# A three-block transformer kernel: causal mask and row minimum of the attentions in one VectorE operation per head and tile, both heads' turned probabilities copied at once, forget logits on quarters of the array

## The chip, the cores and the metric

The kernel runs on one core of a Trainium2 chip. The metric is the device time of one execution in microseconds (us), lower is better. Before the change the median of three runs is 1467.6 us (1465.63 to 1467.93).

## What is computed

Three blocks are applied to 512 tokens of width 1024 in float32: a first block (a gated recurrence, a pooling branch, an MLP of width 4096), a second that mixes 8 heads of attention with a forget gate and 8 heads of retention ("even" in the code, the attention is called fox), and a third with 16 heads in three attention branches ("odd", called nsa). The change touches the softmax of the attentions and the forget gate's logits. Cut to what matters:

```python
# fox: 8 heads of 64, 512 tokens
c = jnp.cumsum(jax.nn.log_sigmoid(f_logit + b_f), axis=1)        # f_logit = h @ w_in[:, 1536:1544]
s = jnp.einsum('bhqd,bhkd->bhqk', qi, kh) * scale
s = s + ci[..., None] - c_h[:, :, None, :]
p = masked_softmax(s, key_pos[None, :] <= t[:, None])            # causal
o = jnp.einsum('bhqk,bhkd->bhqd', p, vh)
# nsa: 16 heads of 64; the selected blocks and the window both cover all 512 tokens here,
# so each of these two branches is a causal softmax with the slope of the head
s = jnp.einsum('bqghd,bgqld->bghql', qi, k_sel) * scale
s = s - slopes * (t[None, None, :, None] - tok)[:, :, None]
p = masked_softmax(s, (tok <= t[None, None, :, None])[:, :, None])
```

## The kernel before, in words

All five engines have an instruction list written out by hand (`@block.tensor` PE, `@block.vector` DVE, `@block.scalar` ACT, `@block.gpsimd` POOL, `@block.sync` SP), and counting semaphores order them. Activations lie in SBUF with 128 features or tokens on the partitions. PE multiplies most weights in three float16 passes (L739 to L741 with weights as the stationary side, L782 to L784 with activations there): a high half times a high half and the two mixed products. SP loads the weights into a ring of three slots, ACT measures (L1364) and makes the high half (L1347), POOL reduces the measure over partitions (L710), DVE makes the low half (L1976). That chain runs ahead of PE through the whole kernel.

`attention(A)` exists on PE, DVE and ACT and is called twice, for fox with 8 heads and one branch (12 steps) and for nsa with 16 heads and two branches (48 steps). A step is one pair of heads (e = 0, 1), one branch and one entry of `TILES`: query tile 3 with 512 keys, or tile 2 with 384 keys, or tiles 1 and 0 together with 256 and 128 keys. Three steps make a round. In each round of the loop over i:

- PE does the scores of step i into PSUM banks 0 to 3 (L960, L964; two slots, so it waits for the exponentials of step i-2), then turns the probabilities of step i-3 into banks 4 and 5, one bank per head (L982), then multiplies the turned probabilities of step i-4 with the values into banks 6 and 7 (L1000). In nsa the first step of a pair of heads also adds the compressed branch (L994).
- DVE adds the constant `future` (1e30 above the diagonal) to the last 128 keys of each tile in PSUM, one operation for both heads (L2521), waits for it, takes the minimum over the keys, again for both heads (L2525), and releases ACT. Scores are negated, so the minimum is the softmax's maximum. Then it takes the reciprocal of the sums of step i-1 (L2534) and scales that step's probabilities (L2543 in nsa, L2541 in fox). Once a pair of heads it multiplies the output by the gate (L2557) and makes a low half (L1890).
- ACT copies the turned probabilities of step i-3 from PSUM to SBUF, one operation per head (L1681), waits for DVE's minimum and makes the exponentials with their sums (L1690), one operation per head and tile.

The order within one engine is fixed by that loop, and the transposes of the two heads wait apart for "probabilities scaled" and "bank free":

```python
975   if TURN_LAG <= i < N + TURN_LAG:
976       s = i - TURN_LAG
977       for e in range(2):
978           pe.wait_ge(s_(n + "_pn"), n_(n + "_pn", 2 * s + e + 1))
979           if s >= 1:
980               pe.wait_ge(s_(n + f"_te{e}"), n_(n + f"_te{e}", s))
```

The forget logits (`fl`, L1217) are 8 columns of weights against 512 tokens: 24 matmuls with 8 stationary columns and 512 moving ones into one bank, and one ACT operation (L1630) that adds the bias. They stand between the projections `vf` and `qr`; the row that comes of them (`frow`) is used only by the fox attention, 100 us later.

## Time and profile before

| | |
|---|---|
| median of three runs | 1467.6 us (1465.63 to 1467.93) |
| the profiled execution | 1465.37 us, its span 1463.5 us |
| PE busy | 1430.4 us, 98% of the span |
| DVE busy | 955.3 us, 65% |
| ACT busy | 860.6 us, 59% |
| chain that ended last | PE 82%, DVE 13%, ACT 2%, issue 1%, DMA 1% |
| costliest lines in the chain | L739 to L741 14% each, L782 to L784 8% each, L2525 4%, L2543 2%, L2521 2% |
| the fox attention | starts at 980 us |
| the nsa attention | starts at 1265 us |

"Busy" is the time in which at least one instruction of the engine is under way. Times of PE are starts; their ends are modelled, so PE counts as busy through short gaps. The chain is followed back from the last instruction; where two engines are about equally loaded it can go through either.

### The profile page before, as it was taken

How to read it: one execution, taken by the hardware profiler on the slowest of the kernel's cores; microseconds unless marked ns; L12 is line 12 of the kernel's file. 1: busy time of each engine (PE TensorE's matmuls, PEld its weight loads, DVE VectorE, ACT ScalarE, POOL GpSimd, SP SyncE). 2: the span in 40 equal slices, each digit the busy share in tenths (PEclk: the TensorE clock that was granted, in tenths of full speed). 3: DMA queues.
4: the chain of work that ended last, by engine and by line, in shares of the span. 5: the costliest groups of instructions: out<-in, count | busy, mean ns of one | idle time of the engine just before them, and what ended most of it. 6: DMA issues, size and time to landing. Idle time of an engine off the chain costs nothing.

```text
span 1463.5 us, 24784 instructions
## 1 busy us (share of the span) xinstructions
PE 1430.4 (98%) x10076; PEld 924.8 (63%) x10076; DVE 955.3 (65%) x1926; ACT 860.6 (59%) x1241; POOL 63.6 (4%) x149
## 2 busy tenths in 40 slices
PE   7999999999999999999999999999999999899998
PEld 4444477556568548576688864746695855366677
DVE  6732556888679675555677524578667337799974
ACT  6554456777564665454563654457655466678863
POOL 0000000000000000000010000100100000000000
PEclk9999999999999999999999999999999999999999
DMA  6323223213332433433232332330223433100002
GB/s 195 107 95 113 88 87 97 76 59 115 100 102 87 136 113 98 141 112 113 95 108 67 113 110 87 96 108 1 61 87 116 144 110 98 58 2 2 2 3 100
DMA packets 128497, 131.85 MB, mean 90 GB/s; under 512 B 9896, under 2 KB 125392, under 8 KB 128256
## 3 DMA queue, kind: packets, MB, share of 16 engines
q1 hardware_dynamic: 126096, 121.62, 26.0%
q0 software_dynamic: 2288, 8.64, 1.7%
q8 instruction: 80, 1.31, 0.4%
q14 instruction: 33, 0.27, 0.1%
HBM read 128.12 MB, written 2.10 MB: 89 GB/s over the span
## 4 chain that ended last, share of the span: by engine, by line
PE 82%; DVE 13%; ACT 2%; issue 1%; DMA 1%; SPq 0%; DVEq 0%; POOL 0%; ACTq 0%
PE bank L739 14%; PE bank L741 14%; PE bank L740 14%; PE bank L782 8%; PE bank L783 8%; PE bank L784 8%; DVE tmin L2525 4%; DVE scr L2543 2%; DVE bank L2521 2%; PE bank L908 1%; PE bank L926 1%; DVE wring L1976 1%; PE bank L1063 1%; PE bank L1158 1%; PE bank L862 1%
## 5 line engine op out<-in xcount | busy, mean ns | idle before, releaser
L739 PE MATMUL bank<-xT,whigh 128*128 128x512 f16 x952 | 361.1, 379 | 0.3 <-DVE wring L1976 0.2
L741 PE MATMUL bank<-xT,wring 128*128 128x512 f16 x952 | 361.1, 379 | 0.0
L740 PE MATMUL bank<-xT,whigh 128*128 128x512 f16 x952 | 361.1, 379 | 0.0
L1976 DVE SCALAR_TENSOR_TENSOR wring<-wring,wsc,whigh 128x2048 f16<-128x2048 f32 (+2 forms) x106 | 245.2, 2313 | 137.1 <-ACT whigh L1347 136.5
L1347 ACT ACTIVATE whigh<-wring,wsc 128x2048 f16<-128x2048 f32 (+2 forms) x106 | 209.0, 1972 | 109.5 <-DVE wsc L1879 90.4
L1364 ACT ACTIVATE whigh<-wring 128x2048 bf16<-128x2048 f32 (+2 forms) x106 | 199.1, 1878 | 92.1 <-DMA wring<-in_w_down 31.2
L782 PE MATMUL bank<-whigh,slab 128*128 128x256 f16 x800 | 218.1, 273 | 1.8 <-DVE wring L1976 1.3
L783 PE MATMUL bank<-wring,slab 128*128 128x256 f16 x800 | 218.1, 273 | 0.0
L784 PE MATMUL bank<-whigh,slab 128*128 128x256 f16 x800 | 218.1, 273 | 0.0
L739 PEld LDWEIGHTS bank<-xT,whigh 128*128 128x128 f16 x952 | 93.2, 98 | 112.8 <-issue 2.7
L741 PEld LDWEIGHTS bank<-xT,wring 128*128 128x128 f16 x952 | 93.0, 98 | 112.5
L740 PEld LDWEIGHTS bank<-xT,whigh 128*128 128x128 f16 x952 | 93.0, 98 | 112.1 <-issue 2.6
L1869 DVE TENSOR_SCALAR wexp<-wexp 128x1 f32<-128x1 f32 x109 | 16.5, 152 | 161.3 <-POOL wexp L710 160.6
L710 POOL PARTITION_ALL_REDUCE wexp<-wsc x109 | 44.6, 410 | 1266.6 <-ACT whigh L1364 1259.8
L1283 ACT ACTIVATE slab<-bank,winv 128x256 f32<-128x256 f32 (+1 forms) x76 | 43.5, 572 | 91.7 <-PE bank L741 50.5
L782 PE MATMUL bank<-whigh,xT 128*128 128x256 f16 (+1 forms) x352 | 89.8, 265 | 0.0
L783 PE MATMUL bank<-wring,xT 128*128 128x256 f16 (+1 forms) x352 | 89.8, 265 | 0.0
L784 PE MATMUL bank<-whigh,xT 128*128 128x256 f16 (+1 forms) x352 | 89.8, 265 | 0.0
L782 PEld LDWEIGHTS bank<-whigh,slab 128*128 128x128 f16 x800 | 78.1, 98 | 12.5 <-issue 3.1
L783 PEld LDWEIGHTS bank<-wring,slab 128*128 128x128 f16 x800 | 78.1, 98 | 9.5
L784 PEld LDWEIGHTS bank<-whigh,slab 128*128 128x128 f16 x800 | 78.2, 98 | 9.2
L1690 ACT ACTIVATE scr<-bank,tmin 128x256 f32<-128x256 f32 (+2 forms) x120 | 61.9, 524 | 28.4 <-DVE tmin L2525 28.2
(335 smaller groups left out, 2270.2 us busy)
## 6 DMA issues: line engine op xcount, KB each, us to landing
wring<-in_w_in SPq DMA_DIRECT2D x27, 1024.0 KB, 5.1
wring<-in_w_up SPq DMA_DIRECT2D x16, 1024.0 KB, 5.4
wring<-in_w_down SPq DMA_DIRECT2D x16, 1024.0 KB, 5.4
wring<-in_even_w_in SPq DMA_DIRECT2D x14, 1024.0 KB, 5.4
wring<-in_odd_w_in SPq DMA_DIRECT2D x14, 1024.0 KB, 5.1
wring<-in_w_a SPq DMA_DIRECT2D x4, 1024.0 KB, 5.4
wring<-in_w_out SPq DMA_DIRECT2D x4, 1024.0 KB, 5.4
wring<-in_even_w_out SPq DMA_DIRECT2D x4, 1024.0 KB, 5.1
```

The costliest lines, as they stand in the source:

```text
L710: pool.partition_all_reduce(wexp[:, n:n + 1], wsc[:, n:n + 1], P, RMAX).then_inc(s_("w_all"), 1)
L739: pe.matmul(bank, wh[:, k, wcol:wcol + width], xh[:, k, :], start=k == 0, stop=False)
L740: pe.matmul(bank, wh[:, k, wcol:wcol + width], xl[:, k, :], start=False, stop=False)
L741: mm = pe.matmul(bank, wl[:, k, wcol:wcol + width], xh[:, k, :], start=False, stop=k == KC - 1)
L782: pe.matmul(bank, xh[:, k, tt], wh[:, k, 0:width], start=k == 0, stop=False)
L783: pe.matmul(bank, xh[:, k, tt], wl[:, k, 0:width], start=False, stop=False)
L784: mm = pe.matmul(bank, xl[:, k, tt], wh[:, k, 0:width], start=False, stop=k == KC - 1)
L1347: act.activation(high_of(i)[:, :, 0:m], loaded(i)[:, :, 0:m], ACT.Copy, scale=wsc[:, n:n + 1]).then_inc(s_("w_high"), 1)
L1364: act.activation(high_of(i)[:, :, 0:m].bitcast(BF16), loaded(i)[:, :, 0:m], ACT.Abs, accum_out=wsc[:, n:n + 1]).then_inc(s_("w_max"), 1)
L1690: ins = act.activation(probs(i, e, SEQ)[:, cc], scores(i, e)[:, cc], ACT.Exp, scale=-1.0, bias=pair_stat(tmin, i, part, e), accum_out=pair ...
L1976: dve.scalar_tensor_tensor(low_of(i)[:, :, 0:m], loaded(i)[:, :, 0:m], wsc[:, n:n + 1], high_of(i)[:, :, 0:m], ALU.mult, ALU.subtract).the ...
L2525: ins = dve.tensor_reduce(pair_stat(tmin, i, part), bank[:, 2 * (i % SCORE_SLOTS):2 * (i % SCORE_SLOTS) + 2, c:c + (t + 1) * P], AX_X, ALU ...
```

## The change

What it does:

- **Mask and minimum.** The constant `future` becomes 128 x 512, zeros in the first 384 columns and the old triangle in the last 128, and its last w columns fit a tile of w keys. One `tensor_tensor_reduce` per head and tile adds it to the scores in PSUM and gives the minimum. Each is two instructions on DVE, the operation and a read of the accumulator. The operation that masked and the one that reduced, each for both heads, go, and so does DVE's wait between them.
- **The constant** is loaded by POOL twice (once ahead of fox into `side` row 9, once ahead of nsa into row 14) and no longer by SP at the start.
- **Copies.** PE signals once when both heads are turned, ACT copies both banks in one operation, and PE waits for that copy before it turns the next step's first head.
- **Forget logits.** 96 matmuls with 8 stationary and 128 moving columns: token tile t goes to the array's columns from 32 t and to its own bank. Four ACT operations of 8 x 128 add the bias, and the bias is loaded by SP to four places.

```diff
-    c["future"] = ((p[None, :] > p[:, None]) * BIG).astype(np.float32)
+    c["future"] = np.concatenate([np.zeros((P, 3 * P)), (p[None, :] > p[:, None]) * BIG], 1).astype(np.float32)
...
-            (future[:, :], cd["future"]),
...
-            (bf_[:, :], a["even_b_f_2"][0].rearrange("(k p) -> k p", p=1)),
+            *((bf_[32 * t:32 * t + 8, :], a["even_b_f_2"][0].rearrange("(k p) -> k p", p=1)) for t in range(TT)),
...
+        future = {"fox": side[:, 9, :], "nsa": side[:, 14, :]}
...
+                    pool.dma_start(future["fox"], cd["future"]).then_inc(s_("decay_in"), 16)
...
+                    pool.dma_start(future["nsa"], cd["future"]).then_inc(s_("nsa_in"), 16)
...
+            def forget_tile(w):
+
+                (wh, wl), (xh, xl) = w, xhalves
+                for k in range(KC):
+                    for n, (ww, xx) in enumerate(((wh, xh), (wh, xl), (wl, xh))):
+                        for t in range(TT):
+                            mm = pe.matmul(SA[t][32 * t:32 * t + 8, 0:P], ww[:, k, 0:8], xx[:, k, t * P:(t + 1) * P],
+                                           start=k == 0 and n == 0, stop=k == KC - 1 and n == 2)
+                mm.then_inc(s_("fl_mm"), 1)
...
                         s = i - TURN_LAG
+                        if s >= 1:
+                            pe.wait_ge(s_(n + "_te"), n_(n + "_te", s))
                         for e in range(2):
                             pe.wait_ge(s_(n + "_pn"), n_(n + "_pn", 2 * s + e + 1))
-                            if s >= 1:
-                                pe.wait_ge(s_(n + f"_te{e}"), n_(n + f"_te{e}", s))
                             for j in range(width(steps[s][2]) // P):
                                 mm = pe.transpose(TPB[e][:, j * P:(j + 1) * P], probs(s, e, SEQ)[:, j * P:(j + 1) * P], ident[:, :])
-                            mm.then_inc(s_(n + f"_tp{e}"), 1)
+                        mm.then_inc(s_(n + "_tp"), 1)
...
-            feat_tile("fl", w, 0, xhalves, SA[0][0:8, :], width=8)
+            forget_tile(w)
...
-            ins = act.activation(frow[0], SA[0][0:8, :], ACT.Identity, bias=bf_[:, 0:1], scale=undo("fl", 0)[0:8, :])
+            for t in range(TT):
+                r = slice(32 * t, 32 * t + 8)
+                ins = act.activation(frow[0][:, t * P:(t + 1) * P], SA[t][r, 0:P], ACT.Identity, bias=bf_[r, 0:1], scale=undo("fl", 0)[r, :])
...
-                        for e in range(2):
-                            act.wait_ge(s_(n + f"_tp{e}"), n_(n + f"_tp{e}", s + 1))
-                            act.activation(turned_probs(s, e)[:, 0:w], TPB[e][:, 0:w], ACT.Copy).then_inc(s_(n + f"_te{e}"), 1)
+                        c = 2 * (s % TURNED_SLOTS)
+                        act.wait_ge(s_(n + "_tp"), n_(n + "_tp", s + 1))
+                        act.activation(xT[:, c:c + 2, 0:w], bank[:, 4:6, 0:w], ACT.Copy).then_inc(s_(n + "_te"), 1)
...
-                        for t, c in steps[i][2]:
-                            last = bank[:, 2 * (i % SCORE_SLOTS):2 * (i % SCORE_SLOTS) + 2, c + t * P:c + (t + 1) * P]
-                            ins = dve.tensor_tensor(last, last, future[:, :].unsqueeze(1).to_broadcast([P, 2, P]), ALU.add)
-                        ins.then_inc(dve_chain, 1)
-                        dve.wait_ge(dve_chain, own(dve_chain))
-                        for part, (t, c) in enumerate(steps[i][2]):
-                            ins = dve.tensor_reduce(pair_stat(tmin, i, part), bank[:, 2 * (i % SCORE_SLOTS):2 * (i % SCORE_SLOTS) + 2, c:c + (t + 1) * P],
-                                                    AX_X, ALU.min)
+                        for e in range(2):
+                            for part, (t, c) in enumerate(steps[i][2]):
+                                w = (t + 1) * P
+                                x = scores(i, e)[:, c:c + w]
+                                ins = dve.tensor_tensor_reduce(x, x, future[n][:, SEQ - w:SEQ], 1.0, BIG, ALU.add, ALU.min, pair_stat(tmin, i, part, e))
                         ins.then_inc(s_(n + "_dm"), 1)
```

Three places show how the instructions move. On DVE in the nsa attention, one step with 512 keys and the next with 384; `tmin` holds the minima, `trec` the reciprocals, `scr` and `side` the probabilities. Before:

```order
L2521 TENSOR_TENSOR bank<-bank,future 128x2x128
L2525 TENSOR_REDUCE tmin<-bank 128x2
L2534 RECIPROCAL trec<-tsum 128x4
L2543 TENSOR_SCALAR scr<-scr,trec,gates 128x256
L2543 TENSOR_SCALAR scr<-scr,trec,gates 128x128
L2543 TENSOR_SCALAR scr<-scr,trec,gates 128x256
L2543 TENSOR_SCALAR scr<-scr,trec,gates 128x128
L2521 TENSOR_TENSOR bank<-bank,future 128x2x128
L2525 TENSOR_REDUCE tmin<-bank 128x2
```

And in the changed kernel (`ISA` is the new operation or, without an input, its accumulator read):

```order
L2534 ISA bank,tmin<-bank,side 128x512
L2534 ISA tmin 128x1
L2534 ISA bank,tmin<-bank,side 128x512
L2534 ISA tmin 128x1
L2542 RECIPROCAL trec<-tsum 128x4
L2551 TENSOR_SCALAR scr<-scr,trec,gates 128x256
L2551 TENSOR_SCALAR scr<-scr,trec,gates 128x128
L2551 TENSOR_SCALAR scr<-scr,trec,gates 128x256
L2551 TENSOR_SCALAR scr<-scr,trec,gates 128x128
L2534 ISA bank,tmin<-bank,side 128x384
L2534 ISA tmin 128x1
L2534 ISA bank,tmin<-bank,side 128x384
```

Two instructions on 2 x 128 and 2 x 512 elements become four on 512, 1, 512 and 1; nothing else on DVE moves. On PE at the forget logits, before:

```order
L784 MATMUL bank<-whigh,xT 128x256
L739 MATMUL bank<-xT,gates 8x512
L740 MATMUL bank<-xT,gates 8x512
L741 MATMUL bank<-xT,gates 8x512
L739 MATMUL bank<-xT,gates 8x512
```

and in the changed kernel, where the projection `qr` follows at once:

```order
L795 MATMUL bank<-whigh,xT 128x256
L751 MATMUL bank<-xT,gates 8x128 x96
L740 MATMUL bank<-xT,whigh 128x512
L741 MATMUL bank<-xT,whigh 128x512
L742 MATMUL bank<-xT,wring 128x512
```

24 matmuls become 96 of a quarter of the length. On ACT in the nsa attention, before:

```order
L1690 ACTIVATE scr,tsum<-bank,tmin 128x128
L1681 ACTIVATE xT<-bank 128x512 x2
L1690 ACTIVATE scr,tsum<-bank,tmin 128x512 x2
L1681 ACTIVATE xT<-bank 128x384 x2
L1690 ACTIVATE side,tsum<-bank,tmin 128x384 x2
```

and in the changed kernel:

```order
L1701 ACTIVATE scr,tsum<-bank,tmin 128x128
L1692 ACTIVATE xT<-bank 128x1024
L1701 ACTIVATE scr,tsum<-bank,tmin 128x512 x2
L1692 ACTIVATE xT<-bank 128x2x384
L1701 ACTIVATE side,tsum<-bank,tmin 128x384 x2
```

The two copies of a step become one of twice the size in the same place of the queue.

## Rows read from the trace of the kernel before

**Rows 1.** 50 us of the nsa attention: busy us of PE, PEld, DVE, ACT, POOL; then clock
```profile
1300.00:1350.00 50.00, 50.00 (x486) 33.57 (x487) 48.69 (x115) 40.97 (x128) 0.00 (x0) 1.00 0.01 2
```
**Rows 2.** Chain that ended last, nsa attention: start, us, what
```profile
1299.68 0.61 DVE slab L2557
...
1370.16 0.61 DVE slab L2557
```
**Rows 3.** Timeline of DVE, one round: start, duration, line, operation
```profile
1338.92 0.42 DVE L2521 TENSOR_TENSOR bank<-bank,future 128x256 f32<-128x256 f32 x1
1339.38 1.23 DVE L2525 TENSOR_REDUCE tmin<-bank 128x2 f32<-128x1024 f32 x1
1340.52 0.17 DVE L2534 RECIPROCAL trec<-tsum 128x4 f32<-128x4 f32 x1
...
1341.89 0.43 DVE L2521 TENSOR_TENSOR bank<-bank,future 128x256 f32<-128x256 f32 x1
...
1343.22 0.15 DVE L2534 RECIPROCAL trec<-tsum 128x2 f32<-128x2 f32 x1
...
1344.33 0.76 DVE L2521 TENSOR_TENSOR bank<-bank,future 128x256 f32<-128x256 f32 x2
...
1346.07 0.15 DVE L2534 RECIPROCAL trec<-tsum 128x2 f32<-128x2 f32 x1
...
1347.04 0.42 DVE L2521 TENSOR_TENSOR bank<-bank,future 128x256 f32<-128x256 f32 x1
```
**Rows 4.** Timeline of PE in the nsa attention
```profile
1314.50 1.07 PE L994 MATMUL bank<-slab 31*64 31x512 f32 x4
...
1341.54 1.09 PE L1000 MATMUL bank<-xT,slab 128*64 128x128 f32 x16
1342.57 0.34 PE L960 MATMUL bank<-side 64*128 64x256 bf16 x4
...
1367.57 1.07 PE L994 MATMUL bank<-slab 31*64 31x512 f32 x4
```
**Rows 5.** Who waited for whom, 1290 to 1390 us: total, times, longest
```profile
PEld bank L982 <- DVE scr L2543: 2.3, 3, 0.8
...
PEld bank L960 <- ACT scr L1690: 0.7, 3, 0.4
```
**Rows 6.** Chain that ended last, fox attention
```profile
989.47 1.22 DVE tmin L2525
...
1007.60 1.23 DVE tmin L2525
```
**Rows 7.** Timeline of ACT in the nsa attention
```profile
1339.00 1.09 ACT L1681 ACTIVATE xT<-bank 128x512 f32<-128x512 f32 x2
1340.64 0.69 ACT L1690 ACTIVATE scr<-bank,tmin 128x512 f32<-128x512 f32 x1 [0.55 <-DVE tmin L2525]
...
1341.32 0.68 ACT L1690 ACTIVATE scr<-bank,tmin 128x512 f32<-128x512 f32 x1
```
**Rows 8.** Instructions of L2301, a running scan in the first block
```profile
L2301 DVE TENSOR_TENSOR_SCAN scr<-segment,scr x8: 1217/1224/1226, 228.4 to 354.9; 128x512 f32<-128x512 f32 x8
```
**Rows 9.** Instructions of L739 on the forget weights: ns least, median, most; first and last start
```profile
L739 PE MATMUL bank<-xT,gates x8: 378/379/380, 870.6 to 875.1; 128*8 128x512 f16 x8
```
**Rows 10.** Timeline of PE in a projection with 128 moving columns
```profile
809.82 0.22 PE L862 MATMUL bank<-xT,slab 128*128 128x128 f16 x1
809.87 0.22 PE L863 MATMUL bank<-xT,slab 128*128 128x128 f16 x1
```
**Rows 11.** Timeline of PE, end of the nsa attention
```profile
1410.35 1.01 PE L982 MATMUL bank<-ident,scr 128*128 128x128 f32 x6 [0.88 <-ACT xT L1681]
```
**Rows 12.** Timeline of POOL after the fox attention
```profile
1052.36 0.60 POOL L710 PARTITION_ALL_REDUCE wexp<-wsc  x1 [22.06 <-ACT whigh L1364]
```
**Rows 13.** Timeline of SP at the start
```profile
18.92 0.36 SPq L634 DMA_DIRECT2D bgate<-in_odd_b_gate  x1
22.89 36.81 SPq L622 DMA_DIRECT2D wring<-in_w_in  x5
```

21 lines of the change are left out of this document (9 added, 12 removed).

## Prediction, made before the changed kernel was run

> **What bounds the kernel now.** The page's table comes first: PE is busy 98% of the span, and the chain runs through it for 82%. So only two kinds of edit can count: one that takes PE time away, and one in a stretch where PE waits or its load is matched by another engine. The forget logits are of the first kind, the attentions of the second, since DVE's 13% of the chain lies mostly there.
>
> Next I read the busy times of a stretch within nsa [rows 1]: PE 50.00 of 50 us, DVE 48.69, ACT 40.97, clock 1.00. Two engines look full, and the question that decides this case is which one sets the pace. The chain goes through DVE, but a chain has to choose. So I measured the period of a pair of heads (two rounds, six steps) on both. DVE's output product comes at 1299.68 and, four pairs later, at 1370.16 [rows 2]: 70.48 / 4 = 17.62 us. PE's compressed-branch product comes at 1314.50 and, three pairs later, at 1367.57 [rows 4]: 53.07 / 3 = 17.69 us. They are equal to 0.4%. The waits agree: in 100 us PE's weight loads waited 2.3 us for DVE's scaled probabilities and 0.7 us for ACT [rows 5], and part of that is under matmuls still streaming. **PE is as full as DVE in nsa**: a faster DVE finds PE at 17.69 us a pair.
>
> Fox is different: the minimum of a pair's first step starts at 989.47 and, two pairs later, at 1007.60 [rows 6], 9.07 us a round. PE's need for a round without L994 follows from nsa: (17.69 - 1.0) / 2 = 8.34, with 1.07 for L994 [rows 4], of which about 1.0 is to the next start. So fox has 0.73 us a round of PE slack.
>
> **The mask and the minimum.** I take DVE's cost from start to start [rows 3]. Step with 512 keys: 1338.92 to 1340.52 = 1.60. Step with 384: 1341.89 to 1343.22 = 1.33. Step with 256 and 128: 1344.33 to 1346.07 = 1.74. Sum 4.67 us of the round of 8.12 (1338.92 to 1347.04). In these, the slope is one element in 1.04 ns, since the reduction of 1024 elements takes 1.14 us to the next start, 1.067 + 0.07. The round's reductions stream 2 x (512 + 384 + 256 + 128) = 2560 elements, 2.67 us, and the masks 1024 more.
>
> The new operations stream the same 2560 elements at best, in 8 operations with 8 accumulator reads. With o the overhead of one operation and its read, the new sum is 2.67 + 8 o, and **break-even is o = (4.67 - 2.67) / 8 = 0.25 us**. The trace has no such operation on DVE. Bounds from the nearest rows: two DVE instructions that don't wait for each other cost 0.07 each, so o = 0.14 at least. At most the read waits until its operation has ended: the reduction of 1024 lasts 1.23 where it streams 1.067 [rows 3], 0.16 over, and a small instruction lasts 0.15, so o = 0.31. The nearest row is ACT's, which has the very pair: an exponential of 512 with its read takes 1341.32 - 1340.64 = 0.68 to the next start, while two copies of 512 without a read last 1.09 together, 0.545 each with the tail of the second [rows 7]. So a read costs ACT 0.14 or a little more. With DVE's 0.07 for the operation that is 0.21, and I take o = 0.2.
>
> DVE then needs 2.67 + 1.6 = 4.27 a round, 0.4 less. In nsa that buys almost nothing, as PE holds 17.69 a pair: I count 0.5 us for PE's visible waits [rows 5] (0 to 0.7). In fox three of the four rounds run in the steady order: 3 x 0.4 = **-1.2** (0 to -2.2, by the 0.73). At the start of each attention DVE's minimum stands alone in the way (nothing is yet there for PE to do), and about 0.25 us each is saved: **-0.5** for both (0 to -0.8). The Trainium skill, in VectorE: DVE Perf Modes, section Rules for kernel authors, speaks against the change: don't fuse chained DVE operations for speed, since the pipeline drains after each, but minimise their number. Here DVE's instructions for mask and minimum rise from 8 to 16 a round; by that rule alone DVE would lose, which is the second rival's time.
>
> **The copies.** ACT's work shrinks by some 0.06 us a step, and ACT is 82% busy in nsa [rows 1]: nothing. But the copy now starts after both heads are turned. In the steady order PE has a product and the scores of the next step between (1341.54 to 1342.57 is the product alone [rows 4]), so the wait is covered by at least 1.7 us of PE work, against 1.0 us of copy; if DVE became late, it would still be covered. At the end of an attention that cover is gone: PE already waits 0.88 us for the first head's copy there [rows 11], and will wait for the whole of it, some 0.45 us more (half of the 1.09 of both copies [rows 7]), twice with a smaller tile after. I count **+0.5** for each attention, +1.0 (0.3 to 1.5).
>
> **The forget logits.** A third of the 24 matmuls of 512 columns start from 870.6 to 875.1 [rows 9], so one takes 4.5 / 21 = 0.214 us and all 5.1 us of a full PE. The 96 new ones have 128 columns, and four in a row go to different columns of the array and different banks. One matmul of 128 columns takes 0.055 to the next start [rows 10]. If none runs beside another, 96 x 0.055 = 5.3: no gain. If four do, 24 x 0.055 = 1.3: gain 3.8. The trace speaks for two beside each other: in L1000, where each head has 64 stationary columns, 16 float32 matmuls of 128 columns take 1342.57 - 1341.54 = 1.03 us [rows 4], 0.064 each, while the transposes, float32 and 128 columns too but on the whole array, take 1.01 / 6 = 0.17 each at most [rows 11]. Whether PE can take 192 instructions (each matmul has a weight load) in 1.3 us isn't shown. I take 2.5 us for the block, nearer to four at once than to none: **-2.6** (0 to -3.8). TensorEngine Tiling (Array Packing) of the Trainium skill, section Theoretical Speedup, gives up to four times, which would be 1.3 us; its section Instruction Overhead has about 60 cycles a matmul, which at 2.4 GHz would be an estimate of 2.4 us for 96.
>
> PE is full from there to 980 us, and the weights are ahead, so this gain carries. The four bias operations on ACT replace one; the row is needed 100 us later.
>
> **Transfers.** POOL issues two more loads. The second is in the list after fox, and POOL then waits 22.06 us for its next work [rows 12]; the first is 200 us ahead of its use. SP issues three more bias loads and one constant less, 0.36 to 0.45 us each, before its next weights; it is idle for 22.89 - 18.92 = 3.97 us there [rows 13]. Nothing.
>
> **Sum.** -2.6 - 1.2 - 0.5 - 0.5 + 1.0 = -3.8 us, so the profiled execution of 1465.37 would become 1461.6. That execution is 2.2 us under the median of 1467.6; against the median the change gives **1463.8 us**. About 0.2% (2.9 us) is what a measurement of this kernel can tell from no change.
>
> **The rivals.**
>
> 1. *Nothing much is gained*: the logits are held by PE's instruction rate, and the attentions by PE. -3.8 + 2.6 = -1.2, 1466.4 us. For it: PE's 17.69, and that nothing shows four at once. Against: L1000's pairs. Chance 0.18.
> 2. *The accumulator read puts DVE over PE* (slower). The place is each step's minimum; it decides from o = 0.25. At o = 0.31 a round of DVE grows by 8 x 0.06 = 0.5 us; 16 rounds in nsa +8.0, 4 in fox +2.0, the starts +0.3, the ends +1.0, the logits -2.6: +8.7, 1476.3 us. For it: ACT's read costs at least 0.14 and may cost more, and DVE has no wait left in nsa that would absorb it. Chance 0.15.
> 3. *The new operation streams at half rate*, as DVE's only operation with a running value here does: the scan takes 1.224 us for 512 elements [rows 8], 2.08 ns each after 0.16. Then 5.33 + 1.6 = 6.93 a round instead of 4.67, 2.26 x 20 rounds = +45, 1511 us with the other terms. Against: the reduction is a running minimum too and takes 1.04. Chance 0.07. The Trainium skill (Vector Engine (DVE) Microarchitecture Reference, Points that are easy to get wrong) says that an operation with accumulator halves its throughput with two float32 SBUF sources; here one source is PSUM.
> 4. *Everything goes well*: o = 0.14, four matmuls at once. -3.8 - 1.5 - 0.8 - 0.7 + 0.5 = -6.3, 1461.3 us. Chance 0.10.
>
> The forecast itself has 0.50, with a range of its own of 1461 to 1467.
>
> **How the numbers follow.** Faster by over 0.2% (under 1464.7): 0.40 of the forecast's 0.50, and rival 4: 0.50. Within 0.2%: the other 0.10 and rival 1: 0.28. Slower: rivals 2 and 3: 0.22. The range reaches down to 1460 for rival 4 with the scatter of the runs, and up to 1473, an o of 0.28; it leaves out rival 3 and the upper half of rival 2.
>
> **What would show it.** The matmuls of the logits: 5.1 us before, near 2.5 after. The operation and read on DVE: from start to start 0.73 for 512 elements if o = 0.2, 0.84 if 0.31, 1.27 at half rate. In nsa the pair's period stays at 17.6 to 17.7, and DVE shows idle time ahead of its minimum, released by PE's scores; in fox the round falls to 8.7. At the ends of the attentions L982 waits more for ACT. I am wrong if the nsa period falls below 17.5, since then PE had slack that its starts hid, or if it rises above 17.8.

## The result, and the profile after

| | before | after |
|---|---|---|
| median | 1467.13 us, 4 runs (1465.63 to 1467.93) | 1457.63 us, 4 runs (1457.29 to 1459.36) |
| ratio after / before | | 0.9941, 95% interval [0.9929, 0.9954] |
| the profiled execution | 1465.37 us, span 1463.5 | 1457.6 us, span 1455.8 |
| chain that ended last | PE 82%, DVE 13%, ACT 2% | PE 90%, DVE 4%, ACT 3% |

The change makes the kernel 0.6% faster, 9.5 us by the medians and 7.7 by the two profiled spans. The forecast was 3.8 us and its range ended 2.4 us above the measured median: right in sign, wrong in size.

I cut both spans at the same places of the program, by the starts of TensorE's first and last matmul of each piece. "Value products" are L1000 before and L1009 after.

| piece, us | before | after | difference | forecast |
|---|---|---|---|---|
| up to the first logits matmul | 870.60 | 871.07 | +0.47 | 0 |
| logits, to the first q product | 5.28 | 1.44 | -3.84 | -2.6 |
| projections up to fox | 103.95 | 103.95 | 0 | 0 |
| fox: first scores to first value product | 11.94 | 11.39 | -0.55 | -0.25 |
| fox: first to last value product | 31.03 | 29.18 | -1.85 | -1.2, and +0.5 at the end |
| between the attentions | 242.29 | 242.92 | +0.63 | 0 |
| nsa: first scores to first value product | 14.68 | 12.36 | -2.32 | -0.25 |
| nsa: first to last value product | 134.82 | 134.47 | -0.35 | -0.5, and +0.5 at the end |
| rest | 48.97 | 49.04 | +0.07 | 0 |

The sum is -7.7. The first piece holds nothing of the change but loads at its start, and it took 870.60, 871.53 and 871.16 us in three profiles of the kernel before, so its +0.47 tells nothing. Between the attentions, where 0 was forecast, TensorE waits for the low halves of weights that DVE makes, a little more than before (engine, line, what it waited for: total, times, longest; from the last value product of fox to the first scores of nsa, before and then after):

```profile
PE bank L782 <- DVE wring L1976: 0.3, 1, 0.3
PE bank L739 <- DVE wring L1976: 0.2, 1, 0.2
```

```profile
PE bank L740 <- DVE wring L1987: 0.8, 3, 0.4
PE bank L793 <- DVE wring L1987: 0.3, 1, 0.3
```

That is 1.1 us against 0.5: part of what the faster fox attention gains is given back there.

**In nsa the engines have changed places as to who waits.** The same 50 us as [rows 1]: PE is as full as it was, DVE has fallen from 48.69 to 42.89 us.

```profile
1300.00:1350.00 50.00, 50.00 (x486) 33.31 (x485) 42.89 (x159) 39.53 (x111) 0.00 (x0) 1.00 0.01 2
```

The waits of the same 100 us as [rows 5] (engine, line, what it waited for: total, times, longest):

```profile
DVE bank L2534 <- PE bank L975: 12.4, 17, 1.1
...
PEld bank L992 <- ACT xT L1692: 6.0, 11, 0.5
```

Before, PE waited for DVE's scaled probabilities and DVE's minimum waited for nothing. Now DVE's new operation waits for PE's scores. The second row is the merged copy: PE's next weight load waits for it, but the engine stays full, as the loads run ahead of the matmuls. The period of a pair has not moved: PE's product of the compressed branch comes at 1324.37, 1342.06 and 1359.75, which is 17.69 us, [rows 4]'s figure to the hundredth.

```profile
1342.06 1.07 PE L1004 MATMUL bank<-slab 31*64 31x512 f32 x4
...
1359.75 1.07 PE L1004 MATMUL bank<-slab 31*64 31x512 f32 x4
```

**The new operation, from start to start.** DVE's timeline of one round of nsa after the change, to hold beside [rows 3]:

```profile
1330.49 0.69 DVE L2534 CUSTOM_DVE_ANT_0 bank<-bank,side 128x512 f32<-128x512 f32 x1
1331.10 0.14 DVE L2534 DVE_READ_ACCUMULATOR2_ANT tmin<- 128x1 f32 x1
1331.10 0.73 DVE L2534 CUSTOM_DVE_ANT_0 bank<-bank,side 128x512 f32<-128x512 f32 x1
1331.74 0.14 DVE L2534 DVE_READ_ACCUMULATOR2_ANT tmin<- 128x1 f32 x1
1331.74 0.17 DVE L2542 RECIPROCAL trec<-tsum 128x4 f32<-128x4 f32 x1
...
1333.12 0.56 DVE L2534 CUSTOM_DVE_ANT_0 bank<-bank,side 128x384 f32<-128x384 f32 x1
...
1334.11 0.16 DVE L2542 RECIPROCAL trec<-tsum 128x2 f32<-128x2 f32 x1
...
1335.84 0.43 DVE L2534 CUSTOM_DVE_ANT_0 bank<-bank,side 128x256 f32<-128x256 f32 x1 [0.53 <-PE bank L975]
1336.19 0.14 DVE L2534 DVE_READ_ACCUMULATOR2_ANT tmin<- 128x1 f32 x1
1336.19 0.33 DVE L2534 CUSTOM_DVE_ANT_0 bank<-bank,side 128x128 f32<-128x128 f32 x1
...
1337.07 0.16 DVE L2542 RECIPROCAL trec<-tsum 128x2 f32<-128x2 f32 x1
```

Look at the starts, not at the durations. Each accumulator read starts at the very time at which the next operation starts: **the read takes no place of its own on the engine**. At most a trace of it is left: the second operation of a step, with a read in front of it, takes 0.64 us to the next start, the first 0.61, and no run tells whether that 0.03 is the read's. The operation costs 0.64 us for 512 elements and 0.25 for 128 (1336.19 to 1336.44, where the next read starts), so one element 1.02 ns and the operation 0.12 us beside them. The three steps of the round take 1331.74 - 1330.49 = 1.25, 1334.11 - 1333.12 = 0.99 and 1337.07 - 1335.84 = 1.23 us, 3.47 against the 4.67 that I had from [rows 3]. In the prediction's form 3.47 = 2.67 + 8 o gives **o = 0.10**, under the lower bound of 0.14. The 1.2 us that a round saves are the 1024 elements that are not streamed again (1.07 us) and DVE's wait between the two old operations (three times 0.12: a mask and its reduction start 0.46 us apart [rows 3], two masks that follow each other 0.33), less 8 x 0.03 for the dearer operations (0.10 against 0.07). The row with a wait shows DVE idle ahead of its minimum, released by PE's scores.

**The logits.** PE's timeline at the logits after the change:

```profile
870.87 0.27 PE L795 MATMUL bank<-whigh,xT 128*128 128x256 f16 x1
871.07 1.51 PE L751 MATMUL bank<-xT,gates 128*8 128x128 f16 x96
872.51 0.39 PE L740 MATMUL bank<-xT,whigh 128*128 128x512 f16 x1
```

96 matmuls and 96 weight loads in 1.44 us, 0.060 for four.

### The profile page after: what moved, and what is told of

The parts are those of the page before. It is cut to its first block, busy times and chain, and to the rows that moved or that the text cites. A ratio compares the mean times of both kernels' runs of the same rounds, so it can differ in the third digit from the quotient of the medians.

```text
span 1455.8 us, 24918 instructions
## 1 busy us (share of the span) xinstructions
PE 1423.5 (98%) x10148; PEld 924.4 (63%) x10148; DVE 936.0 (64%) x2086; ACT 859.1 (59%) x1184; POOL 64.9 (4%) x151
## 4 chain that ended last, share of the span: by engine, by line
PE 90%; DVE 4%; ACT 3%; issue 1%; DMA 1%; SPq 0%; POOL 0%; DVEq 0%; ACTq 0%
PE bank L740 14%; PE bank L742 14%; PE bank L741 14%; PE bank L793 8%; PE bank L795 8%; PE bank L794 8%; PE bank L992 3%; PE bank L1009 3%; PE bank L975 3%; DVE wring L1987 1%; PE bank L919 1%; PE bank L937 1%; PE bank L971 1%; PE bank L1167 1%; PE bank L873 1%
## 5 line engine op out<-in xcount | busy, mean ns | idle before, releaser
L740 PE MATMUL bank<-xT,whigh 128*128 128x512 f16 x952 | 360.8, 379 | 1.6 <-DVE wring L1987 1.6
L740 PEld LDWEIGHTS bank<-xT,whigh 128*128 128x128 f16 x952 | 93.4, 98 | 113.8 <-issue 2.7
L2534 DVE CUSTOM_DVE_ANT_0 bank<-bank,side 128x512 f32<-128x512 f32 (+3 forms) x160 | 74.5, 518 | 15.8 <-PE bank L975 15.4
```

Source lines behind the costliest of these rows:

```text
L740: pe.matmul(bank, wh[:, k, wcol:wcol + width], xh[:, k, :], start=k == 0, stop=False)
L2534: ins = dve.tensor_tensor_reduce(x, x, future[n][:, SEQ - w:SEQ], 1.0, BIG, ALU.add, ALU.min, pair_stat(tmin, i, part, e))
```

## The experiments

Three questions stand behind the runs: what each part of the change is worth alone, by what mechanism, and what the 2.3 us at the start of nsa are. In each comparison the kernel before ran on the same chip beside the others.

### Each part alone

**The logits on quarters alone.**

```diff
-            feat_tile("fl", w, 0, xhalves, SA[0][0:8, :], width=8)
+            forget_tile(w)
...
-            ins = act.activation(frow[0], SA[0][0:8, :], ACT.Identity, bias=bf_[:, 0:1], scale=undo("fl", 0)[0:8, :])
+            for t in range(TT):
+                r = slice(32 * t, 32 * t + 8)
+                ins = act.activation(frow[0][:, t * P:(t + 1) * P], SA[t][r, 0:P], ACT.Identity, bias=bf_[r, 0:1], scale=undo("fl", 0)[r, :])
```

> The kernel before with the forget logits alone on quarters. Theory A (four matmuls of four row groups go side by side, and nothing else of the change is in it): the block from the first logits matmul to the q product falls from 5.28 us to 1.44 us, the time by 3.8 us, to about 0.9974 of before; the attentions are as before. Theory B (the quarters bring 2.6 us, as the prediction had it, and the rest came with the shifted start of what follows): 0.9982. Theory C (a later stage waits for something else and gives it back): 1.000.

Measured: 1463.17 us against 1466.55, ratio 0.9973 [0.9963, 0.9982]. The block is 1.44 us again. (The expectation says row groups; what the four matmuls differ in is the group of columns.) The ratio is worth 4.0 us; 3.8 (theory A) and 2.6 (theory B, 0.9982) are both within the interval or at its edge, so it is the trace that decides for A.

**The mask and minimum in one operation alone.**

```diff
-                        for t, c in steps[i][2]:
-                            last = bank[...]
-                            ins = dve.tensor_tensor(last, last, future[:, :].unsqueeze(1).to_broadcast([P, 2, P]), ALU.add)
...
-                            ins = dve.tensor_reduce(pair_stat(tmin, i, part), bank[...], AX_X, ALU.min)
+                        for e in range(2):
+                            for part, (t, c) in enumerate(steps[i][2]):
+                                w = (t + 1) * P
+                                x = scores(i, e)[:, c:c + w]
+                                ins = dve.tensor_tensor_reduce(x, x, future[n][:, SEQ - w:SEQ], 1.0, BIG, ALU.add, ALU.min, pair_stat(tmin, i, part, e))
```

> The kernel before with the mask and row minimum in one operation alone; copies and logits as before. Theory A (the time after is 7.7 us less, of which the logits are 3.8 and the copies nothing): 3.9 us less, 0.9973 of before: fox attention 2.4 us shorter, the start of the nsa attention 2.3 us shorter, its steady stretch 0.3. Theory B (the merged copies carry part of what the attentions gained, since PE waits for two conditions less a round): at most 1.5 us less, 0.9990. Theory C (the fall of the granted clock at the start of the nsa attention is a matter of where in time it comes, not of this operation): 2.4 us less, 0.9984, with a clock under 0.8 there still.

Measured: 1461.06 us, ratio 0.9964 [0.9951, 0.9977], 5.3 us: more than theory A's 3.9. Fox goes from 11.94 + 31.03 to 11.21 + 28.73 us (-3.03), nsa from 14.68 + 134.82 to 12.51 + 134.05 (-2.94). Both steady stretches are shorter than in the changed kernel (29.18 and 134.47), which theory A did not foresee: something else in the change gives 0.45 and 0.42 us back. Theory C's sign of a fallen clock is there (0.82 and 0.84 from 1265 to 1275 us), and yet the start is 2.2 us shorter; what that is worth is taken up below.

**The merged copies alone**, with TensorE's one signal and one wait a step, as in the change; ACT's side of the edit:

```diff
...
-                        for e in range(2):
-                            act.wait_ge(s_(n + f"_tp{e}"), n_(n + f"_tp{e}", s + 1))
-                            act.activation(turned_probs(s, e)[:, 0:w], TPB[e][:, 0:w], ACT.Copy).then_inc(s_(n + f"_te{e}"), 1)
+                        c = 2 * (s % TURNED_SLOTS)
+                        act.wait_ge(s_(n + "_tp"), n_(n + "_tp", s + 1))
+                        act.activation(xT[:, c:c + 2, 0:w], bank[:, 4:6, 0:w], ACT.Copy).then_inc(s_(n + "_te"), 1)
```

> The kernel before with the turned probabilities of both heads copied at once alone. Theory A (the copy is in nobody's way while VectorE sets the pace, and costs at the ends where the first head's turned probabilities come later): 0 to 1 us more, 1.0000 to 1.0007. Theory B (it carries part of the gain): 1 to 2 us less, 0.9990.

Measured: 1467.57 us, ratio 1.0009 [0.9998, 1.0019]: +1.3 us, the interval just holds 1. Nothing is gained, against theory B. Both stretches from the first to the last value product are those of the kernel before (31.08 us in fox; 135.23 in nsa, where two profiles of the kernel before have 134.82 and one 135.20). In this one profile the time lies elsewhere: 0.67 us between the attentions (242.96), where TensorE waits 0.7 us for DVE's weight halves in projections (L739; 0.2 us before), and 0.74 at the start of fox (12.68), with the clock at 0.50 from 985 to 990 us. Whether the second belongs to the copies one profile can't tell. The three parts add up to -2.7 - 3.6 + 0.9 = -5.4 thousandths; the whole measured -5.9 and, in the comparison further down, -5.5.

### The mechanisms

**The same 96 matmuls, all in one quarter.** Token tile t stays in bank t, but all use the array's first 8 columns.

```diff
-                            mm = pe.matmul(SA[t][32 * t:32 * t + 8, 0:P], ww[:, k, 0:8], xx[:, k, t * P:(t + 1) * P],
+                            mm = pe.matmul(SA[t][0:8, 0:P], ww[:, k, 0:8], xx[:, k, t * P:(t + 1) * P],
...
-                r = slice(32 * t, 32 * t + 8)
+                r = slice(0, 8)
```

> The changed kernel, all its 96 logits matmuls of the same shape but in the same 8 output columns and partitions, each quarter of the tokens still in a bank of its own. Theory A (the gain of the logits is that matmuls of different column groups go side by side): they go one after another, 0.055 us each, the block is 5.3 us again and the time 3.8 us over the changed kernel's, 0.9967 of before. Theory B (the gain is in the number of waits, banks or the copies of the logits): the block stays at 1.4 us and the time that of the changed kernel, 0.994.

PE's timeline at the logits in this run:

```profile
871.53 0.27 PE L795 MATMUL bank<-whigh,xT 128*128 128x256 f16 x1
871.73 5.52 PE L751 MATMUL bank<-xT,gates 128*8 128x128 f16 x96
877.19 0.39 PE L740 MATMUL bank<-xT,whigh 128*128 128x512 f16 x1
```

Measured: 1462.64 us, ratio 0.9973 [0.9964, 0.9983]. The block is 877.19 - 871.73 = 5.46 us long, 96 x 0.057. The number of instructions, of banks and ACT's four operations are those of the changed kernel; only the columns differ. **Four matmuls in four column groups run side by side, and that is all of the 3.84 us.** The run shows it. The prediction's doubt whether PE can take 192 instructions in 1.3 us is answered too: it takes them in 1.44.

**TensorE relieved of 1 us a pair, before and after.** The product of the compressed branch is left out of the output in both.

```diff
-                            if n == "nsa":
-                                for e in range(2):
-                                    pe.matmul(ob[e], vcmp[m % 4][:, m // 2 * HD:(m // 2 + 1) * HD], pcmp(2 * m + e), start=True, stop=True, skip_group_check=True)
...
-                                                   start=n == "fox" and first and j == 0, stop=True,
+                                                   start=first and j == 0, stop=True,
```

> The kernel before without the product of the compressed branch in the output of the nsa attention (TensorE has 1.0 us less to do in a pair of heads; that term of the output is left out). Theory A (VectorE's 17.62 us a pair is as close as TensorE's 17.69): the period stays at 17.6, the steady stretch loses 0.1 to 0.6 us of 134.8 and the time at most 1 us. Theory B (TensorE alone sets the pace before too): the stretch loses 7.5 us, the time 8.

> The changed kernel without the same product of the compressed branch (that term of the output is left out). Theory A (VectorE is no bound any more, since its operation is 0.4 us a round shorter): the period falls by 0.9 to 1.0 us a pair, the steady stretch from 134.5 to about 127, the time by 8 us to 0.9885 of before. Theory B (VectorE's chain, or ScalarE's, stands right behind TensorE): at most 3 us less than the changed kernel, 0.992.

Measured: before without it 1466.68 us, ratio 0.9999 [0.9989, 1.0010]; after without it 1450.83, ratio 0.9894 [0.9880, 0.9908], against the changed kernel's 0.9941. From the first scores of nsa to its last value product it takes 148.40 us in the first (12.24 + 136.16) and 138.99 in the second (11.50 + 127.49), where before and after have 149.50 and 146.83. The stretch between the value products, which theory A of the first had shorter, is 1.3 us longer, as the first value product now comes earlier. The window of [rows 1], in the kernel before without the product and then in the changed kernel without it:

```profile
1300.00:1350.00 50.00, 47.76 (x476) 32.69 (x472) 48.69 (x113) 40.82 (x129) 0.00 (x0) 1.00 0.01 2
```

```profile
1300.00:1350.00 50.00, 50.00 (x506) 34.83 (x505) 45.83 (x170) 42.51 (x117) 0.00 (x0) 1.00 0.01 2
```

Before, TensorE's saved time turns into idle time (50.00 to 47.76 us busy) and DVE stays at 48.69: a pair takes 17.63 us, DVE's own 17.62 of [rows 2]. After, TensorE is full again at once, and the pair takes 16.68 us. The value products of the first step of a round show it, two rounds apart, in the kernel before without the product:

```profile
1315.85 1.09 PE L997 MATMUL bank<-xT,slab 128*64 128x128 f32 x16
...
1333.48 1.09 PE L997 MATMUL bank<-xT,slab 128*64 128x128 f32 x16
```

and in the changed kernel without it:

```profile
1314.07 1.09 PE L1006 MATMUL bank<-xT,slab 128*64 128x128 f32 x16
...
1330.75 1.09 PE L1006 MATMUL bank<-xT,slab 128*64 128x128 f32 x16
```

So before the change two engines stood within 0.07 us of each other in the steady rounds, and neither edit alone could gain there. After it there is 1 us a pair to be had from TensorE.

**The copies head by head again**, in the changed kernel (the diff of the third experiment, the other way round), run twice, the second time beside the changed kernel.

> The changed kernel with the turned probabilities copied head by head again; logits on quarters and the one operation stay. Theory A (the merged copies cost about 1 us at either place: the steady stretches of both attentions were 0.4 us longer with them than in the run with the one operation alone): 0.9 us below the changed kernel, 0.9937 to 0.994 of before, with the stretches at 28.7 us (fox) and 134.05 us (nsa). Theory B (the copies cost only where VectorE sets the pace, and after the change it does not): the time of the changed kernel, stretches at 29.2 and 134.5 us. Theory C (they save where TensorE sets the pace, by one wait less): 1 us more than the changed kernel.

> The changed kernel itself, beside the three others of this comparison. Theory A (the parts add up: logits 3.4 to 3.8, mask and minimum 5.4, copies 1 us the other way): 0.9941 to 0.9950 of before, and 0.8 to 1.0 us above the one with its copies head by head. Theory B (merged copies are free once VectorE is no longer in front): no difference to that one beyond 0.3 us.

> The changed kernel with its turned probabilities copied head by head, once more, beside the changed kernel itself. Theory A (merging delays the first head's value product where no scores stand between, at the end of each attention): the stretches from the first to the last value product are 28.7 and 134.05 us against 29.2 and 134.5, the time 0.8 to 1.0 us less than the changed kernel's, 0.9935 to 0.9944 of before. Theory B: the two times are the same.

Measured: 1458.16 us, ratio 0.9939 [0.9926, 0.9951], the first time; in the direct comparison 1456.90 us, 0.9934 [0.9921, 0.9946], against 1458.22, 0.9945 [0.9933, 0.9958] for the changed kernel. The intervals against before overlap, but the runs themselves hardly do (1456.23 to 1458.22 against 1457.97 to 1460.09), and the stretches are theory A's: 28.73 and 134.05 us, 29.18 and 134.47 in the changed kernel. The starts of the value products of both kernels keep a distance that is constant to 0.01 us for the first 44 groups of nsa and jumps in the last ones alone. PE's timeline there, in the changed kernel (second profile):

```profile
1400.65 0.88 PE L1009 MATMUL bank<-xT,slab 128*64 128x128 f32 x12
1401.68 1.09 PE L992 MATMUL bank<-ident,scr 128*128 128x128 f32 x8 [0.16 <-ACT xT L1692]
1402.70 0.88 PE L1009 MATMUL bank<-xT,slab 128*64 128x128 f32 x12
1404.20 0.87 PE L992 MATMUL bank<-ident,scr 128*128 128x128 f32 x6 [0.63 <-ACT xT L1692]
...
1407.87 0.88 PE L1009 MATMUL bank<-xT,slab 128*64 128x128 f32 x12 [0.15 <-ACT xT L1692]
```

and with the copies apart:

```profile
1400.06 0.88 PE L1011 MATMUL bank<-xT,slab 128*64 128x128 f32 x12
1400.86 1.09 PE L993 MATMUL bank<-ident,scr 128*128 128x128 f32 x8
1401.89 0.88 PE L1011 MATMUL bank<-xT,slab 128*64 128x128 f32 x12
1403.24 1.01 PE L993 MATMUL bank<-ident,scr 128*128 128x128 f32 x6 [0.48 <-ACT xT L1694]
```

Where no scores stand between, the merged copy is waited for three times, 0.94 us, and once, 0.48, when it is apart. Of the 1.3 us between the two medians, 0.87 are these two ends; another 0.47 lies between the attentions (244.80 against 244.33 us, the clock low for a while in both), where TensorE waits 1.3 us for DVE's weight halves against 0.9. **The version with the copies apart is the best of both kernels: the merged copy is a loss of 0.4 us at the end of each attention, and no stretch shows a gain from it.**

### The clock, and the start of nsa

In the profile of before the granted clock is 0.66 from 1275 to 1280 us, which is TensorE at its lower level of 1.2 GHz for part of the window and at 2.4 for the rest, after two gaps of 2.81 and 2.20 us; in that of after it is 1.00 in every window of 5 us from 1260 to 1450 us. So I took part of the 2.3 us for the clock, and filled the gaps with unused matmuls, first in the kernel before, in nsa only:

```diff
+                        if i in (2, 4) and n == "nsa":
+                            if n == "nsa":
+                                pe.wait_ge(s_("ct_ev"), 4)
+                            stat_w, mov = ((sel[:, 0, :], sel[:, 1, :]), (pick[:, 0, :], pick[:, 1, :]))[n == "nsa"]
+                            for _ in range(30):
+                                pe.matmul(ps[7][:, 0:P], stat_w, mov, start=True, stop=True)
```

> The kernel before with 30 more matmuls of 128 columns (results unused) ahead of the scores of the second and third pair in the nsa attention, where TensorE stands idle for 2.8 and 2.2 us. Theory A (of the 2.3 us that the start of that attention lost, some 1 to 1.5 are matmuls at the lower clock after these gaps): the granted clock is 1.00 at 1270 to 1285 us, the start falls from 14.7 us to 13.2, the time by 1 to 1.5 us, 0.9991. Theory B (VectorE sets the end of the start whatever the clock): the start stays at 14.7 us and the time the same, 1.000, or longer by what the matmuls take.

The places are the third and the fifth step of the first pair of heads (i = 2 and 4), not pairs.

Measured: 1465.65 us, ratio 0.9994 [0.9985, 1.0003]. The start is 13.01 us and the clock 1.00 there, as theory A has it, but the steady stretch is 135.30 us in place of 134.82, and the time is the same within what can be measured. Then in all four gaps, in the version with the copies apart and in the kernel before:

```diff
+        WARMTH = {("fox", 2): 24, ("nsa", 2): 26, ("nsa", 4): 20}
...
+                        if (n, i) in WARMTH:
+                            if n == "nsa":
+                                pe.wait_ge(s_("ct_ev"), 4)
+                            stat_w, mov = ((sel[:, 0, :], sel[:, 1, :]), (pick[:, 0, :], pick[:, 1, :]))[n == "nsa"]
+                            for _ in range(WARMTH[n, i]):
+                                pe.matmul(ps[7][:, 0:P], stat_w, mov, start=True, stop=True)
...
+                if half == 1:
+                    for _ in range(32):
+                        pe.matmul(SB[0][:, 0:P], xhalves[0][:, 0, 0:P], xhalves[0][:, 1, 0:P], start=True, stop=True)
```

> The same with copies head by head, and with matmuls of 128 columns whose results are unused in the four gaps of over 1.7 us in which TensorE waits after the logits: 24 ahead of the scores of the third step of the fox attention, 26 and 20 ahead of the third and fifth of nsa, 32 ahead of the second turn of the compressed branch. Theory A (after such a gap the granted clock falls to half in some executions for 2 to 4 us, at each place 1.1 to 1.7 us lost; it fell at the start of fox in every profile): the clock is 1.00 in all windows of 5 us from 975 us on, the time 1.5 to 3 us less than the kernel without them. Theory B (VectorE and ScalarE set the end of the starts, the low clock lies in their shadow): no change beyond 0.5 us, or longer by the added matmuls.

> The kernel before with the same four groups of unused matmuls. Theory A (its share of the gain at the start of nsa, 14.7 us before and 12.4 after, was partly the lower clock): the start is 13.0 us as in the run with one group, no drop of the clock from 975 us on, the time 1.5 to 3 us under before, 0.9985. Theory B (the clock is in the shadow of VectorE, which is slower here than in the changed kernel): the time of before within 0.5 us.

Measured: 1456.64 us, ratio 0.9933 [0.9919, 0.9946], beside 1456.90 without the matmuls; in the kernel before 1468.37, ratio 1.0012 [1.0003, 1.0021], which is slower. The clock was 1.00 in every window around the attentions in both. (It had not fallen at the start of fox in every profile, as the expectation says: with the mask alone it was 1.00 there.) Keeping it up bought nothing measurable, which is theory B's number. The fourth gap, 2.1 us ahead of a turn near 1250 us, is where a fallen clock does cost: the piece between the attentions took 242.3 to 243.0 us in the seven profiles without added matmuls there in which the clock stayed up, and 244.0 to 244.8 in the eight in which it fell behind this gap (0.66 to 0.98 in one or two windows of 5 us). With the matmuls it was 243.30 and 244.36 at full clock, for TensorE then stood waiting for DVE's weight halves instead (2.4 us in the kernel before, on L740 and L783; 1.4 in the other). That is where the kernel before lost: 2.07 us more between the attentions than in its first profile, against 1.20 less in nsa. What delays the weight halves isn't settled.

Last, the kernel before twice more and the new operation alone once more, each unchanged, one profile each.

> The kernel before itself, for a second profile. In the five profiles of kernels with the old mask and minimum the start of the nsa attention took 14.7, 13.2, 13.7, 13.0 and 13.0 us, the last two with added matmuls and no drop of the clock; in those with the new operation 12.3 to 12.5, whatever the clock. Theory A (the operation saves some 0.7 to 1.2 us there, and the rest of the 2.3 is how deep and where the clock falls in the one execution): 13.0 to 13.8 us here. Theory B (the start is 2.3 us shorter by the operation, whatever the clock): 14.7 us again.

> The kernel before once more, for a third profile. Theory A: the start of the nsa attention takes between 13.0 and 14.7 us, by where and how long the granted clock is under 0.9 in it. Theory B: 14.7 us.

> The kernel before with the new operation for mask and minimum alone, for a second profile. Theory A (with the shorter operation the start hides a lower clock): 12.3 to 12.6 us for the start of the nsa attention and 11.2 to 11.4 for fox, whether the clock falls or not. Theory B (it varies as with the old operation): 12.5 to 14 us.

Measured, with all profiles of kernels that compute the whole output (start and steady stretch of nsa, us):

| mask and minimum | copies | runs | start | steady | sum |
|---|---|---|---|---|---|
| old | apart | before, before again (first) | 14.68, 14.67 | 134.82, 134.82 | 149.5 |
| old | apart | before again (second), logits alone | 13.11, 13.24 | 135.20, 135.21 | 148.3, 148.5 |
| old | merged | copies alone | 13.72 | 135.23 | 149.0 |
| old | apart | both with added matmuls | 13.01, 13.01 | 135.30, 135.29 | 148.3 |
| new | apart | mask alone twice, both with copies apart | 12.37 to 12.51 | 134.05 | 146.4 to 146.6 |
| new | apart | copies apart, with added matmuls | 12.27 | 134.05 | 146.3 |
| new | merged | after, after again, one quarter | 12.36 to 12.51 | 134.47 | 146.8 to 147.0 |

The kernel before has two courses. In one, TensorE's clock falls late, after the gap ahead of the fifth step's scores, and the matmuls up to the first value product, which comes at 1279.76, run at the lower level (the profile of before):

```profile
1275.45 0.34 PE L960 MATMUL bank<-side 64*128 64x384 bf16 x2 [2.20 <-ACT scr L1690]
1275.61 1.44 PE L964 MATMUL bank<-slab 64*128 64x384 f32 x4
1276.98 1.54 PE L982 MATMUL bank<-ident,scr 128*128 128x128 f32 x6
1278.46 1.37 PE L994 MATMUL bank<-slab 31*64 31x512 f32 x4
```

In the other it falls earlier, after the gap ahead of the third step's scores, and the fifth step's groups run at full rate (the kernel before, third profile, with its first value product at 1280.42):

```profile
1273.70 0.67 PE L960 MATMUL bank<-side 64*128 64x512 bf16 x2
1274.12 1.86 PE L964 MATMUL bank<-slab 64*128 64x512 f32 x4
1275.92 1.09 PE L982 MATMUL bank<-ident,scr 128*128 128x128 f32 x8
1277.69 0.34 PE L960 MATMUL bank<-side 64*128 64x384 bf16 x2 [0.68 <-ACT scr L1690]
1277.86 0.82 PE L964 MATMUL bank<-slab 64*128 64x384 f32 x4
1278.61 0.87 PE L982 MATMUL bank<-ident,scr 128*128 128x128 f32 x6
```

In both, the fifth step's scores wait for exponentials of the third and come 10.4 us after the first scores (1275.45 - 1265.08 and 1277.69 - 1267.31), so the low clock on the third and fourth step costs nothing. From there to the first value product it is 4.31 us in the late course and 2.73 in the other; 0.4 us of the difference comes back in the steady stretch, and **the late course costs 1.2 us over the other** (149.5 against 148.3).

So of the 2.7 us that nsa lost between the two first profiles (149.50 to 146.83), 1.2 are the late fall in the one of before. **The operation's own share, with the copies apart and the clock full, is 148.3 - 146.3 = 2.0 us** (the two kernels with added matmuls: 13.01 + 135.29 against 12.27 + 134.05), and the merged copies give 0.4 back. The first of the last three profiles gave theory B's 14.7, outside theory A's range, and the second 13.11, theory A's, so it is A's mechanism with two courses; the third gave 12.50 and 11.21 us, theory A's numbers. What they do not show is that the new operation hides a late fall. In its eight profiles without added matmuls the clock fell early (down to 0.66 in a window of 5 us) or not at all, and an early fall costs the kernel before at most 0.2 us too (0.7 with the copies merged, where the clock was low for longer). Whether the operation keeps the clock from falling late or eight profiles missed it stays open.

Nor is the late course a slower kernel: it was seen only where the clock had stayed up near 1250 us. From the last value product of fox to that of nsa the kernel before takes 391.8 us in the late course (two profiles) and 392.3 in the other (the third), since what the one loses at the start of nsa the other loses behind the gap near 1250.

## Why the prediction was wrong, and where it was right

**Right: the steady rounds of nsa.** "PE is as full as DVE in nsa": from the 7th to the 45th group of nsa's value products, 1297.8 to 1408.6 us, the kernel before and the one with the new operation alone keep a distance of 3.97 us, constant to 0.01. A DVE that needs 1.2 us a round less gained nothing there. The period of 17.6 to 17.7, the idle time ahead of DVE's minimum and its releaser came out as written.

**Right: the copies**, +1.0 (0.3 to 1.5) forecast. The direct comparison gives 1.3 us by the medians and 0.45 + 0.42 = 0.87 at the ends of the attentions, where it was forecast; the rest lies between them, in waits for weight halves that the prediction put at nothing. What I had not seen is that the ends need the faster DVE: in the kernel before with the copies merged alone, both stretches are unchanged (beside the third profile of the kernel before, nsa loses 0.22 us at its end and has made up 0.37 near its start). That DVE's old minimum hides part of the copy there is my reading; one profile stands behind it.

**Wrong: o, the overhead of the new operation and its read.** In the forecast's sum, mask and minimum are -1.2 - 0.5 - 0.5 = -2.2 us; the stretches show 2.30 + 0.73 in fox and 0.74 + 1.24 in nsa, 5.0 us. The step that failed first is "two DVE instructions that don't wait for each other cost 0.07 each, so o = 0.14 at least", and then the choice of 0.2 by ACT's pair. Measured o is 0.10. The lower bound gave the read a place of its own; on DVE it starts together with the operation that follows. It was also wrong to call 0.14 a bound: it was an estimate of two prices, one of them of an instruction that the trace did not hold. A rival with DVE's read free belonged on the list; instead two rivals had the operation dearer than I took it. With o = 0.10 a round is 1.2 us shorter on DVE, not 0.4. Rivals 2 and 3 (o at 0.31, half rate) are refuted by the rows above.

The Trainium skill's rule against the change (VectorE: DVE Perf Modes, section Rules for kernel authors) stood in the prediction: don't fuse chained operations, minimise their number. Here the measurement speaks against it: the number of instructions rose from 8 to 16 a round and the time fell from 4.67 to 3.47 us, by the three terms worked out above. The page Perfetto Trace Analysis (section Optimizing Scalar/DVE Operations) of the Trainium skill gives DVE about 125 ns of overhead an operation on PSUM; the 0.12 us beside the elements of the new operation agrees; the reductions on PSUM, with 0.07 [rows 3], lie under it.

**Wrong: fox.** -1.2 (0 to -2.2) was forecast for the steady rounds and -0.25 for the start. The new operation alone brings -2.30 and -0.73. With o = 0.10 DVE's round would be 9.07 - 1.2 = 7.87, under PE's 8.34, so PE's slack of 0.73 is used up: that was the forecast's own upper end. The value products of the first step of each round, fox, before:

```profile
991.76 1.09 PE L1000 MATMUL bank<-xT,slab 128*64 128x128 f32 x16
...
1000.10 1.09 PE L1000 MATMUL bank<-xT,slab 128*64 128x128 f32 x16
...
1009.23 1.09 PE L1000 MATMUL bank<-xT,slab 128*64 128x128 f32 x16
...
1018.05 1.09 PE L1000 MATMUL bank<-xT,slab 128*64 128x128 f32 x16
```

and with the new operation alone:

```profile
992.19 1.09 PE L1001 MATMUL bank<-xT,slab 128*64 128x128 f32 x16
...
1000.53 1.09 PE L1001 MATMUL bank<-xT,slab 128*64 128x128 f32 x16
...
1008.87 1.09 PE L1001 MATMUL bank<-xT,slab 128*64 128x128 f32 x16
...
1016.18 1.09 PE L1001 MATMUL bank<-xT,slab 128*64 128x128 f32 x16
```

The distances are 8.34, 9.13, 8.82 before and 8.34, 8.34, 7.31 now. "Three of the four rounds run in the steady order" was wrong in its form: the first round was at PE's pace already, the second gives the 0.79 of PE's slack, and the third 1.51, and it holds turns and value products of the attention's end, where no scores keep PE busy; that DVE sets the pace there is read from this. The end, which I had priced for the copies alone, was worth as much to the operation.

**Wrong: the start of nsa and the ends.** I priced the start with one minimum, 0.25 us. It has two in the way, the first step's and the third's (the second's runs beside the first step's exponentials): with the clock full in both, the third step's minimum starts 0.28 us sooner after the first scores (6.67 and 6.39 us), its exponentials 0.73 (8.51 and 7.78), and the start goes from 13.01 to 12.27 us, 0.74. In the steady stretch, from 135.29 to 134.05, the gain lies in the six groups behind the first (0.84 us) and ahead of the last but one (0.40); in between, it is zero. Another 1.2 us between the two first profiles was the place at which the clock fell, on which the prediction has no term.

**Wrong: the logits**, the term that was mis-sized. 2.6 of 3.84. "I take 2.5 us for the block, nearer to four at once than to none": it is 1.44, my own other end of 1.3 and a little. The doubt was whether PE issues 192 instructions in that time. The Trainium skill's TensorEngine Tiling (Array Packing), section Instruction Overhead, has some 60 cycles a matmul, by which 96 would take an estimated 2.4 us at 2.4 GHz; the trace disagrees where four groups of columns are in use: 0.015 us a matmul, 36 cycles. Its section Theoretical Speedup (up to four times) agrees: 5.28 / 1.44 = 3.7.

**The range.** My rival 4, with all well, gave 1461.3 and the range ended at 1460. The terms of the gain came out at or beyond their good ends, because those of the attentions were estimates that I treated as bounds; the copies alone came out dear. The upper end doesn't follow from my own sums either: an o of 0.28 gives some 20 x 0.24 = 4.8 us more by DVE and, with rival 2's other terms, about 1471 and not 1473. (SP's 3.97 us of [rows 13] is from start to start; idle it is for 3.6, which changes nothing.)

## What to carry to other kernels

Take a shared limit as a limit of the steady rounds only: where two engines are equally full, a faster one gains nothing in the middle and gains at the start, at the end and in any round that lacks the other's work (here 2.0 us in nsa). Count those rounds one by one, and ask what stands right behind them: here some of the gain went to waits for weights. And when a cost is not in the trace, the bound of "how cheap can it be" is zero unless a row excludes it. Where a merging of operations delays the first half, look at the rounds without cover; that it pays where its own engine sets the pace no run here tried.

## What the runs showed of the hardware

- DVE's accumulator read starts together with the next operation and takes at most 0.03 us from start to start, though it is listed with 0.14 us. ACT's does take time: from its start to the next exponential's it is 0.09 us (1332.85 to 1332.94 in the profile of after), of the 0.66 us that an exponential of 512 elements with its read takes to the next start.
- DVE's custom operation with two sources, one of them in PSUM, with write-back and running minimum, streams float32 at 1.02 ns an element (0.64 us for 512, 0.25 for 128), as fast as the reduction alone (1.04).
- Four 128-column matmuls in four column groups and four banks start within 0.010 us of each other and take 0.060 us together (1.44 / 24). The same four in one group take 0.228 (5.46 / 24).
- A granted clock that falls after a gap of 2 us costs by what waits for the matmuls behind it: 1.7 us ahead of a projection (243.98 against 242.29 between the attentions), 1.2 us at the start of nsa on the fifth step and at most 0.2 on the third and fourth (0.7 in a profile where it was low for longer). At the start of fox the time was 11.94 us with a window of 5 us at 0.66 (before) and 11.95 with the clock at 1.00 throughout (before with added matmuls); 12.12 to 12.13 and, with the clock low for longer, 12.68 us were seen as well.
